# Two waits added to the relative-bias map that GpSimd builds, in a two-block transformer kernel on one Trainium2 core

## What is computed

```python
dist = positions[:, q0:q1, None] - positions[:, None, :q1]
bias = rel_bias[_t5_bucket(dist)].transpose(0, 3, 1, 2)[:, :, None]
logits = jnp.einsum('bhmqd,bhmkd->bhmqk', q, k) * scale + bias
```

## Time and profile before

| | us |
|---|---|
| median of 3 runs | 2360.46 |
| lowest, highest | 2359.82, 2362.37 |
| the profiled execution, its own time | 2362.72 |
| its span in the trace | 2361.4 |
| PE busy | 2257.7 |
| DVE busy | 1501.5 |
| ACT busy | 954.9 |
| POOL busy | 367.7 |

### The profile page before, as it was taken

The page is one execution under the profiler, slowest core; times in us unless marked ns, Lnnn a source line. Parts: engine busy times, 40 slices in busy tenths (PEclk is TensorE's granted clock), DMA queues, the critical chain, the costliest instruction groups (busy, mean ns, idle before and its releaser), DMA issues. The chain is left out here.

```text
span 2361.4 us, 36947 instructions
## 1 busy us (share of the span) xinstructions
PE 2257.7 (96%) x14328; PEld 1914.6 (81%) x14328; DVE 1501.5 (64%) x2311; ACT 954.9 (40%) x1534; POOL 367.7 (16%) x365
## 2 busy tenths in 40 slices
PE   6999999999999999999999999979999999998998
PEld 4888887666678888878888876669998998898998
DVE  4666766565675666666565346556667766876874
ACT  4222223455442222242222244545446334555763
POOL 1000001000000000000000010039995476000000
PEclk9999999999999999999999999999999999999999
DMA  7554445111134444434443242124544232244544
GB/s 280 190 189 178 171 165 178 72 37 54 54 134 160 168 175 170 169 119 178 160 177 129 98 129 80 55 87 154 191 168 167 94 115 73 90 146 158 179 175 144
DMA packets 52615, 331.03 MB, mean 140 GB/s; under 512 B 6545, under 2 KB 7825, under 8 KB 21649
## 3 DMA queue, kind: packets, MB, share of 16 engines
q1 hardware_dynamic: 49040, 319.15, 37.4%
q0 software_dynamic: 3456, 10.25, 1.5%
HBM read 325.56 MB, written 3.80 MB: 139 GB/s over the span
## 5 line engine op out<-in xcount | busy, mean ns | idle before, releaser
L1183 PE MATMUL bank<-u_hi,whi 128*128 128x512 f32 (+1 forms) x2512 | 867.6, 345 | 32.5 <-DVE u_lo L1137 14.9
L1184 PE MATMUL bank<-u_lo,whi 128*128 128x512 f32 (+1 forms) x2512 | 848.7, 338 | 0.0
L1185 PE MATMUL bank<-u_hi,wlo 128*128 128x512 f32 (+1 forms) x2512 | 848.1, 338 | 0.0
L568 DVE TENSOR_TENSOR wlo<-raw,whi 128x2048 fp32r<-128x2048 f32 (+2 forms) x207 | 433.3, 2093 | 317.0 <-ACT whi L566 317.0
L1183 PEld LDWEIGHTS bank<-u_hi,whi 128*128 128x128 f32 x2512 | 477.2, 190 | 108.9 <-issue 29.5
L1185 PEld LDWEIGHTS bank<-u_hi,wlo 128*128 128x128 f32 x2512 | 477.5, 190 | 51.6
L1184 PEld LDWEIGHTS bank<-u_lo,whi 128*128 128x128 f32 x2512 | 477.8, 190 | 48.8 <-issue 0.2
L566 ACT ACTIVATE whi<-raw 128x2048 fp32r<-128x2048 f32 (+2 forms) x207 | 353.1, 1706 | 340.6 <-PE bank L1185 254.0
L1245 ACT ACTIVATE sil<-bank 128x512 f32<-128x512 f32 (+1 forms) x88 | 47.8, 544 | 541.7 <-PE bank L1185 541.7
L1183 PE MATMUL bank<-hidden_hi,whi 128*128 128x512 f32 x528 | 205.4, 389 | 0.0
L1184 PE MATMUL bank<-hidden_lo,whi 128*128 128x512 f32 x528 | 205.4, 389 | 0.0
(11 more groups left out here) (426 smaller groups left out, 2907.2 us busy)
## 6 DMA issues: line engine op xcount, KB each, us to landing
raw<-in_stream SPq DMA_DIRECT2D x231, 1024.0 KB, 4.8
raw<-in_stream SPq DMA_DIRECT2D x80, 704.0 KB, 4.0
first_ada<-in_stream SPq DMA_DIRECT2D x8, 1024.0 KB, 16.4
raw<-in_stream SPq DMA_DIRECT2D x8, 768.0 KB, 4.3
skew<-rpb_rows POOLq DMA_DIRECT2D x8, 336.0 KB, 6.2
nbr_bias<-skew POOLq DMA_DIRECT2D x24, 112.0 KB, 3.5
h<-in_tokens SPq DMA_DIRECT2D x1, 2048.0 KB, 11.5
uq_ukv<-in_small POOLq DMA_DIRECT2D x1, 1536.0 KB, 8.0
```

The lines of the kernel that those rows point to most:

```text
L568: v.tensor_tensor(self.lo[to][:, 0:n], raw[:, 0:n], self.hi[to][:, 0:n].bitcast(F32), ALU.subtract).then_inc(self.s_lo, 1)
L1183: pe.q.matmul(dst, w[0], x[0], start=start, stop=False)
L1184: pe.q.matmul(dst, w[0], x[1], start=False, stop=False)
L1185: return pe.q.matmul(dst, w[1], x[0], start=False, stop=stop)
```

## The change

Two entries in a table of waits: ahead of bucket 0 POOL waits until PE has finished two panels of the second layer's `up2`, and ahead of bucket 15 until PE has finished the first panel of `rwkv_in`. The same function is used for buckets 20 to 30, which have no entry. Nothing else differs; all instructions and their order on each engine stay.

```diff
@@ -1349,11 +1349,13 @@
             z = pool.do(pool.q.tensor_scalar(rel[:, hh, :], dist[:, :], 0.0, table[:, hh, 0:1], ALU.mult, ALU.add))
         return bias_steps(z, range(BIAS_FIRST), range(DH))
 
+    map_waits = {0: (st.s_pe, PHASE[("up2", L1 - 1)].first + 2), 15: (st.s_pe, PHASE["rwkv_in"].first + 1)}
+
     def bias_steps(z, buckets, heads_):
 
         for b in buckets:
             start = float(bucket_starts()[b])
-            pool.after(z)
+            pool.after(z, map_waits.get(b))
             z = pool.do(pool.q.tensor_scalar(bucket[:, :], dist[:, :], start, start - 1.0, ALU.min, ALU.max))
             for hh in heads_:
                 pool.after(z)
```

## The result

The changed kernel takes 2365.61 us, median of 20 runs (2359.1 to 2369.41), against 2359.81 for the kernel before, median of 20 runs beside them (2357.91 to 2362.81): a ratio of 1.0026 [1.0020, 1.0032], 5.8 us slower. The forecast was 2357.8, in a range that ended at 2361.2. Together the two pauses pay what was forecast; the moved buckets cost about 9 us instead of 1.1.

What follows compares the result with a forecast made beforehand. PE was taken to bound the kernel, with time to gain only where it waits, around the norms and in block two's first stage. -3.3 - 0.5 + 1.1 = -2.7 us gave a median of 2357.8, range 2354.2 to 2361.2.

Steps and rivals of the forecast that it cites:

- Part 1: First pause, around the norm after `out`: DVE freed of POOL, a gain of 3.3 us, bounds 1.5 and 5.
- Term (a): In `out`, the first L589 gets 0.8 us shorter while PE stands for it: 0.8 us gained, all on the path.
- Term (b): From there to the last update of `h`: a second L589 gives 0.8, three L995 give 0.7, together 1.5 us.
- Term (c): The first norm's chunks, first multiply to last low part, get shorter without POOL: 1.0 us taken as gain.
- Part 2: Second pause, last third of the norm before `rwkv_in`: from 8.8 towards 8.3 us, gain 0.5, bounds 0 and 1.2.
- rival (A): Around 1580 to 1585, PE's shorter stand also keeps its clock up: -5 to -6 us, 2355.0; chance 0.2.
- When POOL will run: Timing: bucket 0 moves to about 1611, bucket 14 ends near 1795, buckets 15 to 19 run from 1804.5 to 1855-1865.5.
- Rival (D): Bucket 14 ends after 1804.5, so the second pause never happens: 2358.3; counted inside the forecast's 0.55.
- Part 3: Five buckets moved into block two's first stage slow two L568 and four L2235: 1.1 us lost, bounds nothing and 5.7.
- Rival (C): Block two's first stage: DVE loses every collision, plus a clock drop; +1.9 to +3.6 us, 2362.4 to 2364.1; chance 0.1.
- Parts at nothing: Wait instructions, bucket 20 at worst 7.5 us late (covered by L2403's 11.4 us wait), SP's queue and feed-forwards: no cost.
- The signs of being wrong: Wait at 1852.58 growing by over 2 us, L2403's wait gone, or the two norms as long as before.

Runs made afterwards that it cites:

- second_only: The changed kernel with only the wait ahead of bucket 15 kept, no wait ahead of bucket 0: 2366.59 us, 1.0033 of the kernel before.
- the memsets: The changed kernel with both pauses, buckets 15 to 19 replaced by 90 POOL memsets that read nothing: 2357.26 us, 0.9992 of the kernel before.
- second_at_4: The changed kernel with the second pause lasting until the fourth panel of `rwkv_in`, whole map kept: 2366.50 us, 1.0026 of the kernel before.
- early_8: Against the kernel before, eight buckets run early beside the second layer's attention, then one pause until `up2`'s second panel: 2357.83 us, 0.9991.

## Why the prediction was wrong

**Parts 1 and 2 were right, in mechanism and size.** Part 1 said 3.3, the traces show 3.4, and the L589 take 1.22 us as it said. Term (a) was 0.8: PE's stand ahead of `out`'s last panel went from 2.59 to 1.77 us, against "1.8 or less". Term (b) was 1.5: from the second update of `h` behind that stand (L1293) to the last (L1302) DVE takes 6.2 us for 7.7, of which one L589 is 0.8 and the L995 are 0.7. Term (c), the chunks, was put at 1.0 and is 0.6 (9.6 us went to 9.0). What is missing there is made up by luck: 0.4 us that the sum did not have, 0.15 ahead of that second update and 0.25 between the last update and the first multiply. Part 2 said 0.5 and 8.3 us were left of 8.8. The runs bear the sum out: with no bucket in block two's first stage the kernel gains 3.4, 3.8 and 4.5 us against the forecast's 3.8.

**What rival (A) named did occur, and paid next to nothing.** Before, PE was granted 0.67 of full speed in 1580 to 1585, right after the stand. In the changed kernel the same work begins at 1577.66:
```profile
1577.00:1582.00 5.00, 4.34 (x36) 4.37 (x36) 3.48 (x7) 1.79 (x3) 0.00 (x0) 1.00 0.58 210
```
The clock stays at 1.00. The same split runs through all twelve profiled executions: in the kernel before and in `second_only`, with stands of 2.59 and 2.58 us, it falls to 0.50 here; in the ten others, with 1.75 to 1.78, it does not. But PE does not set the pace in this place: behind the first of these updates of `h` none waits for PE in either kernel, so the time that the clock gives back is waited away for DVE. The 5 to 6 us of rival (A) did not come.

**"When POOL will run" was right.** Bucket 0 was expected near 1611 and started at 1606.1; the pauses were 31.3 and 12.1 us for 34 and 10. Rival (D) did not occur.

**Part 3 is the step that failed:** "Sum: 1.1 us lost". The measured loss is 9.3 us, outside its own bounds of nothing to 5.7. What the runs showed in its place: 5.3 us more of waiting on PE, behind DVE's whole queue of short steps, and about 3.9 us of lower clock. Three things were wrong in it.
- *It took a list of instructions for the path.* It went through "the places where PE has no slack" in the kernel before, found two L568, one copy and four L2235, and stopped. DVE's scans, `kk`, `bonus` and L2166 were no such places, since DVE had slack there: ahead of the L568 of 1823.40 it stood idle for 0.54 us. But between 1819.06 and 1829.6 it had nearly no other gap, so what these instructions lose adds up: 3.9 + 1.0 + 0.8 + 1.4 + 1.4 + 0.75 = 9.25 us, of which some 0.5 is taken up by the gap by 1831. `v_tokens` and the copy behind them reach PE late. The chain was read at its end instead of over DVE's queue.
- *It took a price per instruction from wide, isolated ones.* 0.26 us was the mean over 21 L568 of 2.29 us. The bound even gave each L2235 a whole POOL instruction, but the many short instructions in a row were left out. For their length they suffer most: a scan has 190 ns of its own and lost 244 on average, sixteen times over.
- *It said that what is lost "comes back at 1852.58".* The wait of 2.67 us was indeed absorbed, but PE stood for 3.70 and 3.94 us further up, and the clock was at 0.50 at the end of both; it fell three times instead of once, which by the estimate above cost 3.9 us besides the 5.3 of waits.

**Rival (C) was right in its mechanism and wrong in its price.** It named collisions in block two's first stage lost by DVE, with drops of the clock behind them, and priced them at 5.7 + 1.7 = 7.4; it got one chance in ten, on the ground that the same L568 beside POOL costs 0.25 us on average. That row is true and was no evidence for short instructions. The Trainium skill ("SBUF — State Buffer", section "Who interferes with whom") was named beside it. It says that a DVE instruction with two SBUF inputs and a GpSimd instruction that reads SBUF exclude each other, and that a GpSimd instruction that only writes does not contend with it. By that rule the sum was to be a loss of 1 to 2 us; the runs go further in its direction, and the memsets agree with both halves of it (scans 3.03 beside a writing POOL, 6.95 beside a reading one). That one engine stands wholly still while the other runs is not to be seen in the records: in the 6.95 us of the scans POOL is busy for 6.2. The Trainium skill's statement in the same section, that a `tensor_scalar` can run in a mode that takes both ports, is in agreement with `kk` at 1.86 beside the memsets, though no run here tells which mode it was in.

**"Parts at nothing" were right for the kernel changed.** The wait for `uq_ukv` was to shrink and stayed at 11.5 us; it is used up where the second pause ends three panels later (`second_at_4`).

**The signs of being wrong were not the right ones.** The wait at 1852.58 was to grow, the wait at L2403 to be gone, or the norms to be as long as before. None of this happened, and the kernel was slower all the same: every sign looked at the places that the sum had, and the loss lay between them.

**What stays open.** An order of DVE's work that would keep the wide `wlo` and the short steps apart was not tried. The 3.9 us of clock are an estimate from one execution of each kernel. When the clock falls is not explained: in this stage it fell with stands of 3.70, 3.94 and (`early_8`) 3.0 us and stayed at 1.00 with stands of 2.80 (the memsets) and 2.67 (the kernel before), but the one fall of the kernel before follows no stand of over 0.5 us.

## What to carry to other kernels

A pause for a helper engine is worth what it frees, less what its work meets where it lands, so check the landing place first: here a stage in which DVE and PE hand work back and forth took 9.3 us for the 3.9 that two norms gave. Price contention over the whole queue of the engine between two of its idle gaps, and do not take the price of a short instruction from a wide one: the scans doubled while wide subtractions beside the same work lost a tenth on average. If the work must go somewhere, look for a stretch where the disturbed engine has slack. Beside the second layer's attention DVE was busy for 8.5 us more and PE's busy time did not change, and five buckets moved there gave 4 us, with one pause instead of two.

## What was not expected of the hardware

Sixteen scans of 64 elements went from 3.03 to 6.95 us beside POOL instructions that read SBUF and stayed at 3.03 beside POOL instructions that only write. Four-fold `tensor_scalar` steps with one SBUF operand and a scalar were stretched by both, from 1.14 to 2.55 and to 1.86.

Where PE never waits and the granted clock is 1.00, the same matmuls ran at two speeds. Busy time in 1640 to 1680 of the kernel before, then of the changed one:
```profile
1640.00:1680.00 40.00, 40.00 (x353) 39.83 (x352) 25.81 (x23) 19.12 (x23) 37.34 (x30) 1.00 0.56 197
```
```profile
1640.00:1680.00 40.00, 40.00 (x344) 39.95 (x343) 26.13 (x23) 18.06 (x23) 37.24 (x31) 1.00 0.52 185
```
That is 353 matmuls in 40 us, 113 ns each, against 344, 116 ns; the other profiled kernels had 340 to 345. In both traces the starts of matmuls lie either 113 or 118 ns apart: 118 in the changed kernel at 1640 and 113 at 1670, 113 in the kernel before at both and 118 at 1690. From the last L1153 of the first norm to the first multiply of the second it is 190.7 us before and 191.8 after, so the profiled execution of before was quick here by about 1 us. The cause is open; the medians over 20 runs do not hang on it.
